# Head norms: mean squares with the tokens on the partitions, and a second matmul that spreads the roots over the features

## What is computed

```
y = x32 * lax.rsqrt(jnp.mean(x32 * x32, axis=-1, keepdims=True) + EPS)
return (y * w.astype(jnp.float32)).astype(x.dtype)
```

## Time and profile before

| | |
|---|---|
| median of 3 runs | 1190.63 us (1189.59 to 1196.57) |
| profiled execution | 1190.49 us, span 1188.7 us |
| PE busy | 1091.9 us, 92% of the span |
| DVE busy | 787.0 us, 66% |
| ACT busy | 610.2 us, 51% |
| POOL busy | 170.5 us, 14% |
| mean granted TensorE clock | 0.973 |

### The profile page before, as it was taken

How to read it: one execution, slowest core, us unless ns; L and a number is a source line. 1 busy time by engine, 2 the same in 40 slices (tenths; PEclk the granted TensorE clock), 3 DMA queues, 4 the chain that set the end, 5 groups by cost and what they waited for, 6 DMA issues and landing times.

```text
span 1188.7 us, 23717 instructions
## 1 busy us (share of the span) xinstructions
PE 1091.9 (92%) x8466; PEld 1037.2 (87%) x8466; DVE 787.0 (66%) x1290; ACT 610.2 (51%) x1074; POOL 170.5 (14%) x186
## 2 busy tenths in 40 slices
PE   5999989999998987779999999988788898999999
PEld 5978879999998776679999999987677788999999
DVE  7664676666555785776665658867755648888853
ACT  7643554444544554364444546665544447666542
POOL 4000121111110001031111100000101003444400
PEclk9999989999999998889999999999988999999999
DMA  7522345555664222055555664442222236555563
GB/s 265 176 93 94 92 152 197 185 180 174 190 186 155 77 93 67 27 171 191 179 182 177 181 202 143 163 139 89 89 71 72 78 118 195 179 185 185 168 197 114
DMA packets 52775, 174.45 MB, mean 147 GB/s; under 512 B 5856, under 2 KB 9056, under 8 KB 52576
## 3 DMA queue, kind: packets, MB, share of 16 engines
q1 hardware_dynamic: 52704, 173.49, 45.3%
HBM read 172.42 MB, written 1.05 MB: 146 GB/s over the span
## 4 chain that ended last, share of the span: by engine, by line
PE 50%; DVE 12%; ACT 2%; issue 2%; POOL 0%; ACTq 0%; DVEq 0%
PE bank L561 15%; PE bank L562 15%; PE bank L563 15%; DVE ring_lo L1220 2%; PE bank L614 1%; DVE xw_lo L1226 1%; DVE bank L1367 1%; DVE bank L1365 1%; DVE u L1383 1%; DVE x L1275 1%; DVE negmax L1429 1%; PE bank L700 1%; ACT tmp L1054 1%; PE bank L627 1%; DVE tmp L1426 1%
## 5 line engine op out<-in xcount | busy, mean ns | idle before, releaser
L561 PE MATMUL bank<-xw_hi,ring_hi 128*128 128x256 f32 x1736 | 508.7, 293 | 8.2 <-DVE xw_lo L1226 3.4
L562 PE MATMUL bank<-xw_lo,ring_hi 128*128 128x256 f32 x1736 | 495.4, 285 | 0.0
L563 PE MATMUL bank<-xw_hi,ring_lo 128*128 128x256 f32 x1736 | 495.0, 285 | 0.0
L1220 DVE TENSOR_TENSOR ring_lo<-ring_raw,ring_hi 128x1024 fp32r<-128x1024 f32 (+3 forms) x353 | 399.9, 1136 | 50.1 <-ACT ring_hi L838 43.6
L838 ACT ACTIVATE ring_hi<-ring_raw 128x1024 fp32r<-128x1024 f32 (+3 forms) x353 | 345.0, 979 | 101.1 <-PE bank L563 97.0
L561 PEld LDWEIGHTS bank<-xw_hi,ring_hi 128*128 128x128 f32 x1736 | 337.9, 195 | 17.3 <-issue 10.1
L562 PEld LDWEIGHTS bank<-xw_lo,ring_hi 128*128 128x128 f32 x1736 | 337.7, 195 | 4.1 <-issue 3.9
L563 PEld LDWEIGHTS bank<-xw_hi,ring_lo 128*128 128x128 f32 x1736 | 337.1, 194 | 0.0
L561 PE MATMUL bank<-act_hi,ring_hi 128*128 128x256 f32 x848 | 250.1, 295 | 29.5 <-DVE ring_lo L1220 11.7
L562 PE MATMUL bank<-act_lo,ring_hi 128*128 128x256 f32 x848 | 245.2, 289 | 0.0
L563 PE MATMUL bank<-act_hi,ring_lo 128*128 128x256 f32 x848 | 244.9, 289 | 0.0
(11 more groups left out here) (159 smaller groups left out, 854.6 us busy)
## 6 DMA issues: line engine op xcount, KB each, us to landing
ring_raw<-w_up SPq DMA_DIRECT2D x132, 512.0 KB, 3.2
ring_raw<-w_in SPq DMA_DIRECT2D x85, 512.0 KB, 3.2
ring_raw<-w_down SPq DMA_DIRECT2D x48, 512.0 KB, 3.7
ring_raw<-w_down SPq DMA_DIRECT2D x24, 384.0 KB, 3.9
ring_raw<-w_oa SPq DMA_DIRECT2D x16, 384.0 KB, 3.1
ring_raw<-w_kv SPq DMA_DIRECT2D x8, 512.0 KB, 5.7
ring_raw<-w_oa SPq DMA_DIRECT2D x8, 512.0 KB, 3.5
ring_raw<-w_ob SPq DMA_DIRECT2D x16, 128.0 KB, 2.0
```

What stands on the lines that cost most here:

```text
L561: mm(bank[b][:, 0:T], w_hi, tile(hi, t), start=kk == 0, stop=False)
L562: mm(bank[b][:, 0:T], w_hi, tile(lo, t), start=False, stop=False)
L563: last = mm(bank[b][:, 0:T], w_lo, tile(hi, t), start=False, stop=end)
L1220: V.tensor_tensor(ring_lo[:, a:b], ring_raw[:, a:b], ring_hi[:, a:b].bitcast(f32), SUB).then_inc(lo_done, 1)
```

## The change

The squares are made as before. PE then uses the squares as the stationary operand: four matmuls, each with 128 tokens of one tile as 128 weight columns and a moving operand of 2 columns (`means64` or `means128`). Bank 4 then holds 8 columns with the tokens on the partitions: for each of the four token blocks the mean square of the tile's two heads. ACT's log and exp and DVE's Newton step run on these 8 columns, in a small buffer `norm_tok`. A new step, `spread`, brings the roots back: eight matmuls, each with one column of roots, broadcast 64 times, as stationary operand and the 128x128 identity as moving operand, so that 64 partitions of bank 4 get the root of each token. DVE's last multiplication reads bank 4 instead of the buffer.

The steps move too. The Newton step is now the DVE step `norm`, a LATE one in slot s+1 (its log and exp on ACT were there already); `spread` is the first step of PE in slot s+2; `norm_out` stays in slot s+3, EARLY, with one operation left; `norm_soon` is still in slot s+2, but a LATE step now, behind L1220. Two 128-column constants are gone and two 2-column ones came.

```diff
         at(layer, slot + 1, "norm", tile)
+        plan[layer][slot + 2].insert(0, ("spread", tile))
         if soon:
-            plan[layer][slot + 2].insert(0, ("norm_soon", tile))
+            at(layer, slot + 2, "norm_soon", tile)
...
-                mm(bank[4][:, :], cmat(SPEC[layer, t][0]), normed(n), start=True, stop=True).then_inc(np_ms, 1)
+                for d in range(4):
+                    last = mm(bank[4][:, 2 * d:2 * d + 2], normed(n)[:, d * P:(d + 1) * P], cmat(SPEC[layer, t][0], 2),
+                              start=True, stop=True)
+                last.then_inc(np_ms, 1)
...
+            def spread(layer, t):
+                n = norm_no(layer, t)
+                pe.wait_ge(np_nt, 3 * n + 3)
+                y = of_norm(norm_tok, n)
+                for d in range(4):
+                    for half in range(2):
+                        root = y[:, 2 * d + half:2 * d + half + 1].to_broadcast([P, 64])
+                        last = mm(bank[4][64 * half:64 * half + 64, d * P:(d + 1) * P], root, cmat("ident"),
+                                  start=True, stop=True)
+                last.then_inc(np_bc, 1)
...
-                roots(norm_no(layer, t), 512, scale, e)
+                roots(norm_no(layer, t), of_norm(norm_tok, norm_no(layer, t)), scale, e)
...
+            def norm(layer, t):
+                n = norm_no(layer, t)
+                y = of_norm(norm_tok, n)
+                v = newton_step(n, y)
+                V.scalar_tensor_tensor(y, v, -3.0 / SPEC[layer, t][1], y, ADD, MUL).then_inc(np_nt, 1)
+
             def norm_out(layer, t):
-                v, y = newton_step(n, 512)
-                V.scalar_tensor_tensor(y, v, -3.0 / scale, y, ADD, MUL).then_inc(np_nt, 1)
-                dve.wait_ge(np_nt, 3 * n + 3)
+                dve.wait_ge(np_bc, number["stat", (layer, t)] + 1)
...
                     last = V.scalar_tensor_tensor(u[:, a * T:(a + 2) * T], u[:, a * T:(a + 2) * T], pcol(name, k),
-                                                  normed(n), MUL, MUL)
+                                                  bank[4][:, :], MUL, MUL)
...
-            MIDDLE = {"norm_soon", "group_out"}
+            MIDDLE = {"group_out"}
```

More of the change, by code:

```diff
@@ L69 @@
 NPARAM = _at
[L72 to L73 removed]
+CONSTS = [("ident", 128), ("ones1024", 128), ("ones512", 128),
+          ("dist", 384), ("distT", 384), ("causal", 128), ("pick", 32), ("means64", 2), ("means128", 2)]
 CCOL, _at = {}, 0
@@ L101, in constants @@
     put("causal", causal)
+    put("means64", np.kron(np.eye(2), np.full((64, 1), 1 / 64)))
+    put("means128", np.full((P, 2), 1 / 128))
     put("pick", np.kron(np.eye(2), np.tile(np.eye(32)[:, :16], (2, 1))))
@@ L435, in program @@
                     count("norm" if kind == "group_norm" else kind, (kind, *k) if kind in ("norm", "group_norm") else k)
+                    if kind == "norm":
+                        count("stat", k)
                     if kind == "values" and filled(layer, key[0], key[1])[1]:
@@ L439, in program, with of_norm @@
                         count("biased", k)
+        def of_norm(buf, n):
+            return buf[:, (n % 2) * 8:(n % 2) * 8 + 8]
         def norm_no(layer, t):
@@ L786, in ssd_out @@
                 last.then_inc(ss_y, 1)
-            DO = {"norm": norm, "group_norm": group_norm, "turn": turn, "ret_scores": ret_scores, "ret_out": ret_out,
+            DO = {"norm": norm, "spread": spread, "group_norm": group_norm, "turn": turn, "ret_scores": ret_scores, "ret_out": ret_out,
                   "scores": scores, "weights": weights, "values": values, "cb": c_times_b, "small": small_steps,
@@ L949, in squares, with roots @@
                 A(normed(n), u[:, a * T:(a + 2) * T], ACT.Square).then_inc(np_sq, 1)
-            def roots(n, width, scale, e):
+            def roots(n, y, scale, e):
+                width = y.shape[1]
                 act.wait_ge(np_ms, n + 1)
-                A(normed(n)[:, 0:width], bank[4][:, 0:width], ACT.Ln, scale=scale, bias=eps(e)).then_inc(np_ln, 1)
+                A(y, bank[4][:, 0:width], ACT.Ln, scale=scale, bias=eps(e)).then_inc(np_ln, 1)
                 act.wait_ge(np_ln, n + 1)
-                A(normed(n)[:, 0:width], normed(n)[:, 0:width], ACT.Exp, scale=-0.5).then_inc(np_rt, 1)
+                A(y, y, ACT.Exp, scale=-0.5).then_inc(np_rt, 1)
             def norm(layer, t):
                 _, scale, e, _, _ = SPEC[layer, t]
-                roots(norm_no(layer, t), 512, scale, e)
+                roots(norm_no(layer, t), of_norm(norm_tok, norm_no(layer, t)), scale, e)
             def group_norm(layer, g):
@@ L963, in group_norm @@
                 act.wait_ge(np_out, n - 1)
-                roots(n, T, 1.0, 0)
+                roots(n, normed(n)[:, 0:T], 1.0, 0)
             def turn(layer, t):
@@ L1357, in ssd_conv, with newton_step @@
                     other_taps("conv4", 4, j, j, j % 2, two(conv_out, j % 2))
-            def newton_step(n, width):
+            def newton_step(n, y):
                 dve.wait_ge(np_rt, n + 1)
-                v, y = bank[4][:, 0:width], normed(n)[:, 0:width]
+                v = bank[4][:, 0:y.shape[1]]
                 V.scalar_tensor_tensor(v, v, eps(0), y, ADD, MUL).then_inc(np_nt, 1)
@@ L1368, in newton_step @@
                 dve.wait_ge(np_nt, 3 * n + 2)
-                return v, y
+                return v
+            def norm(layer, t):
[3 more added lines that the diff above has]
+                V.scalar_tensor_tensor(y, v, -3.0 / SPEC[layer, t][1], y, ADD, MUL).then_inc(np_nt, 1)
             def norm_out(layer, t):
-                n = norm_no(layer, t)
                 _, scale, _, name, k = SPEC[layer, t]
-                v, y = newton_step(n, 512)
-                V.scalar_tensor_tensor(y, v, -3.0 / scale, y, ADD, MUL).then_inc(np_nt, 1)
-                dve.wait_ge(np_nt, 3 * n + 3)
+                dve.wait_ge(np_bc, number["stat", (layer, t)] + 1)
                 a = t % 64
@@ L1380, in norm_out @@
                         last = V.scalar_tensor_tensor(tile(u, a + s), tile(u, a + s), pcol(name, k + s),
-                                                      two(normed(n), s), MUL, MUL)
+                                                      bank[4][:, s * T:(s + 1) * T], MUL, MUL)
                 else:
                     last = V.scalar_tensor_tensor(u[:, a * T:(a + 2) * T], u[:, a * T:(a + 2) * T], pcol(name, k),
-                                                  normed(n), MUL, MUL)
+                                                  bank[4][:, :], MUL, MUL)
                 last.then_inc(np_out, 1)
@@ L1388, in group_out @@
                 n = number["norm", ("group_norm", layer, g)]
-                v, y = newton_step(n, T)
+                y = normed(n)[:, 0:T]
+                v = newton_step(n, y)
                 V.scalar_tensor_tensor(y, v, -3.0, y, ADD, MUL).then_inc(np_nt, 1)
@@ L1536, in ssd_gate @@
                 V.tensor_tensor(y, y, tile(u, t), MUL).then_inc(ss_g, 1)
-            DO = {"norm_out": norm_out, "norm_soon": norm_out, "group_out": group_out, "ret_scores": ret_scores, "gated": gated, "scores": scores,
+            DO = {"norm": norm, "norm_out": norm_out, "norm_soon": norm_out, "group_out": group_out, "ret_scores": ret_scores, "gated": gated, "scores": scores,
                   "softmax": softmax, "values": values, "small": small_steps, "ssd_weights": ssd_weights,
```

20 lines of the change are left out of this document (10 added, 10 removed).

## The result

The changed kernel takes 1173.12 us (median of 4 runs, 1171.6 to 1173.7); before, timed beside it, took 1192.09. The ratio is 0.984, with a 95% interval of 0.980 to 0.987. Timed once more for the experiments it took 1173.54. The profiled execution has a span of 1171.1 us against 1188.7.

What follows compares the result with a forecast made beforehand. It took PE's waits on DVE around the norms as the bound. 3.3 + 11.6 + 2.0 - 4.0 - 2.4 = 10.5 us won, plus 7 of clock, total 17.5, gave 1173 us; range 1158 to 1194.

Steps and rivals of the forecast that it cites:

- First group: PE's waits for norm_out itself: 11 waits, 14.3 us, of which 3.3 us would be won after PE's added work.
- Second group: PE's waits for something behind a norm_out in the same EARLY place: six norms, 11.6 us won.
- a wait of length W is filled with E first: PE's added work fills a wait behind a shorter DVE chain; won is the smaller of 2.24 us and W - E.
- E: Net added PE time per norm: mean square 0.70 plus spread 1.15 minus removed 0.86, 1.0 us (bounds 0.86 and 1.9).
- Third group: Two of L561's three waits for POOL, for layer 1's mixed heads out of norm_soon: 1.0 us each, 2.0 won.
- The clock: Stretches behind shrunken waits in the two attention stages regain granted clock: between 0 and 14 us, taken as 7.
- LATE costed at nothing: The small Newton step, 0.67 us on DVE in an earlier slot's LATE, costs nothing, except in two slots.
- the 2.4 us of slots 10 and 14: In layer 1, log, exp and Newton step stand before the next softmax: 1.2 us lost in each slot.
- The uncovered norms: Tiles 24, 37, 39 (layer 0) and 6 (layer 1), without a PE wait, pay E: 4.0 us lost.
- Rival 1: The spread's two halves on PE don't overlap, so E is 1.9 us: 1194 us, chance 0.15.
- Rival 2: The spread, first in a slot's PE steps, waits for its Newton step and delays the rest: 1212 us, chance 0.08.
- Rival 3: Waits shrink but the clock gains nothing, or tiny matmuls lower it elsewhere: 1180 to 1184 us, chance 0.11.

Runs made afterwards that it cites:

- e_slow: The changed kernel with three more 512-column operations on DVE in norm_out (EARLY), ahead of its multiplication: 1212.99 us, ratio 1.018 to the kernel before.
- e_late: The changed kernel with three more 512-column DVE operations in LATE, directly behind the small Newton step: 1189.13 us, ratio 0.999 to the kernel before.
- e_order: The changed kernel with the step norm at the head of slots 10 and 14 of layer 1, ahead of the score maps: 1168.46 and again 1168.58 us.
- e_move: The kernel before with its three 512-column Newton operations moved from norm_out to LATE of slot s+1, no spread: 1180.54 us, ratio 0.991.
- e_old: e_order with four norms (tiles 24, 37, 39 of layer 0, tile 6 of layer 1) back in the old form: 1166.37 us.
- e_both: e_order with norm_soon back in DVE's MIDDLE place, ahead of the low part of the weights: 1171.13 us.

## Why the prediction was right

The time was forecast at 1173 and is 1173. The mechanism held: the waits behind DVE's shorter EARLY place shrank, PE paid about 1.0 us a norm, and some clock came back. That the hit is so exact is luck, for two terms were missed by 3 to 4 us each and offset each other: the pauses shrank less than forecast, and more clock came back.

- **Pauses.** The sum of 10.5 contains 24 x 1.0 us of PE's work, so it forecast 34.5 us fewer pauses. Measured 31.4. First group: all 11 waits on norm_out vanished, but the one of 2.1 us ahead of the scores came back in the softmax waits of the same heads, which rose from 1.5 to 3.3 and from 0.9 to 1.3 or 2.0. Second group: L627, L620, L700 and L724's 3.5 were to lose 17.6 (11.6 and 6 x 1.0) and lost 5.6 + 2.2 + 3.4 + 1.9 = 13.1. The step that was off is "a wait of length W is filled with E first": e_slow shows that E fills much less than that. Third group: the two waits for POOL lost 2.6 each (to 0.7 and 2.2), 2.0 were forecast.
- **PE's work.** E was put at 1.0 and is about 1.0, out of two terms that were both off: the mean square 0.81 to 0.91 instead of 0.70, the spread 0.92 to 1.03 instead of 1.15. L761's row was a poor guide to the mean square; why, no run shows. By the Trainium skill (TensorE: Matmul & The Clock Gate, LDWEIGHTS) an estimate for eight loads is 0.86; the trace agrees with that, at 0.81 to 0.91.
- **The clock.** Mechanism right, size too small: 7 forecast, 10.7 by the account. In layer 2 six stretches at half clock became three in both profiles, not all behind the same waits. e_slow shows how much hangs on it: of what DVE's shorter EARLY place is worth there, 16 of 37 us are clock.
- **LATE costed at nothing.** The three small operations take 0.57 us each norm, as forecast (0.67). At e_late's 0.31 that is about 4 us in all, an estimate; the 2.4 us of slots 10 and 14, of which e_order shows about 1.0 without the clock, are a part of it. That the cover was thin I had seen for these two slots only; e_move shows what happens to whoever takes it as given.
- **The uncovered norms** cost 3.3 us in layer 0, where 3.0 were forecast, and 0.6 for tile 6, where it was 1.0 (e_old).
- **Rival 1** fell: the halves overlap although they share all rows (1.03 against 1.51). The Trainium skill (same page, The mechanism) names another row group, or the spare weight buffer, as what lets a load overlap; this trace shows that with all rows shared the order of the column halves decides too. **Rival 2** is seen at its mildest: the spread waits for its Newton step in slots 11 and 15 of layer 1, for 0.75 to 0.93 us. **Rival 3**'s remark that waits of 1 to 2 us remain is true, but the clock stays up behind most of those (behind the one of 1.87 us in layer 2 it fell in three of the six profiles of the changed kernel, e_order, e_both and e_old).
- DVE's and ACT's busy times fell by 36.3 and 20.4 us; 38 and 20 were forecast. ACT's shorter log and exp were not tested by themselves; e_slow keeps them and shows none of the gain.

## What to carry to other kernels

Work on an engine that is busy 66% of the time can cost more than work on one that is busy 92%: in front of what PE waits for, a us of DVE cost 0.81 us, in the place behind its own slot's work 0.31, and a us of PE 0.95 once the waits were gone, but 0.86 at most while they stood (21.0 us for 24.5 in e_slow). So price an operation by its place, not by its engine; and before moving one to a "free" place, look at what stands behind it there. The change won because it shrank the moved operations fourfold; moving them alone won 11 us where both won 18. Where the clock falls behind a pause, the pause costs nearly twice its length (37 us for 21 of pauses in e_slow).

## What the runs showed of the hardware

- The clock fell behind pauses and not from the kind of matmul: the same PE program lost 17.6 or 19.9 us at half clock in the changed kernel, 26.1 in e_late and 37.5 in e_slow. But a pause's length alone doesn't say whether it falls. Six profiles (two of the changed kernel, two of e_order, e_both, e_old) have the same program and the same pauses in layer 2: half clock stood behind the waits of 3.32 and 2.99 us in all six, behind that of 1.87 in three, behind that of 2.18 in one, and behind that of 1.67 in none. In the kernel before, a wait of 3.31 us left the clock at 2.4 GHz.
- Eight float32 matmuls of 128 columns into alternating 64-partition halves take 1.03 us, one half after the other 1.51.
- A DVE or ACT operation on 8 columns costs far more than its share of 512 columns. The groups, in the columns of the earlier trace rows:

```profile
L977 ACT ACTIVATE norm_tok<-bank,par 128x8 f32<-128x8 f32 x24 | 6.4, 266 | 31.3 <-PE bank L624 31.2
...
L1389 DVE SCALAR_TENSOR_TENSOR bank<-bank,par,norm_tok 128x8 f32<-128x8 f32 x24 | 5.6, 232 | 8.7 <-ACT norm_tok L979 8.5
...
L979 ACT ACTIVATE norm_tok<-norm_tok 128x8 f32<-128x8 f32 x24 | 5.0, 209 | 0.8
...
L1399 DVE SCALAR_TENSOR_TENSOR norm_tok<-bank,norm_tok 128x8 f32<-128x8 f32 x24 | 4.0, 166 | 0.8
```

266 and 209 ns on ACT where 512 columns took 689 and 631; 232 and 166 ns on DVE where they took about 0.75 and 0.69 us. A line through 256 and 512 columns had given the sums of these to within 0.1 us (0.67 for DVE's three, 0.57 measured; 0.49 for ACT's two, 0.48 measured).
